# Small vectors, conditions, signal, router and filter inputs as a few column arrays, with the head of the Hyena mixer reordered

## The chip, the core and the metric

The kernel runs on one core of one Trainium2 chip, as one launch. The metric is the device time of one execution in microseconds (us). Inputs lie in the device's main memory when the execution begins, and laying them out in another order on the host, before the launch, is not in the time.

## What is computed

One inference step of a two-layer model on two token streams, in float32: 128 context tokens and 256 latent tokens of width 1024. The streams are kept side by side as 384 token columns. Layer 0 mixes tokens with a bidirectional Hyena long convolution, layer 1 with a bidirectional RG-LRU scan, and each is followed by a mixture of 16 experts (two per token). Each sub-layer is preceded by an RMS norm and modulated by vectors that come from the condition vectors `c` and `c_ctx`:

```
silu_c = silu(cond)
for i in range(2):
    mod = (silu_c @ ada_w[i] + ada_b[i])          # 1024 x 6144 weights
    sh1, sc1, g1, sh2, sc2, g2 = split(mod, 6)
    h = rms_norm(x, norm_mix[i]) * (1 + sc1) + sh1
    m = hyena_mixer(h) if i % 2 == 0 else rglru_mixer(h)
    x = x + g1 * m
    h = rms_norm(x, norm_moe[i]) * (1 + sc2) + sh2
    x = x + g2 * moe_ffn(h)                       # scores, top-2 experts, w1, w3, w2
```

The Hyena filter comes from a small network on fixed positional features, `h = sin(freq * (z @ f_w1 + f_b1))`, `h = sin(freq * (h @ f_w2 + f_b2))`, `h @ f_w3`. Its output is multiplied by a decaying window, normalised, and taken to its spectrum.

## The kernel before, in words

Each engine runs its own instruction list, and the lists are ordered by hand. Semaphores tie them: `wait_ge` holds back one engine's list, and `then_inc` releases. Two engines issue DMAs: SyncE (the rows SPq) and ScalarE (the rows ACTq). A DMA issued by ScalarE stands in ScalarE's list, ahead of the arithmetic that follows it.

**SyncE** loads the two condition vectors as 8 rows each and the identity (lines 353 to 356), the third filter weight `w3` in two halves (L365), and then the stream of weight pieces of 1 MB: eight `ada_w` pieces at once, then `hy_w_in` and further `ada_w` pieces, each after a wait on `ada_mm` or `in_mm0`, which TensorE raises when it is done with a piece's buffer (L374 to L391). After that come the expert weights of 2 MB each (L344).

**ScalarE** first issues ten small DMAs for the filter network (L439 to L444; three vectors of 64 values, each loaded twice, four bytes a partition), then the two signals into `h` (L446, L447), the constants (L448), the window (L449) and the cosine tables `lags` (L450). It computes the sigmoid of the conditions (L452), issues 16 DMAs that bring the small vectors as rows of 128 values into `hT` (L463), then the router weight with 64 bytes a row (L465), and the router bias spread over all partitions (L466). Only then does the filter network's first `sine` begin (L475 to L482): an `Identity` activation into `f_arg` (L478), a range reduction on VectorE (`reduced`, L1245 to L1258), and the `Sin` (L481). Then four evictions of transposed signal tiles (L472), the second `sine`, two copies that build `stack` (L488, L489), the eight squares of the first norm (L495) and its square root (L497).

**TensorE** transposes the conditions (L755), waits for all ten filter DMAs, does the first filter matmul, `ada(0, 1)`, the transposes of the signal (24 tiles of 128x128, from `h` to PSUM), the second filter matmul, the four transposes of the small vectors, `ada(2)`, and `filter_rows(0)`, which needs `stack` and `w3`. `ada(n)` multiplies the conditions with one 1 MB piece: 4 matmuls, 8 records in the trace. In `mixer0` (L923 on) follow `norm_sums(0)`, which needs the eight squares, `ada(3)`, `spectrum(0)`, `norm_spread(0)`, `filter_sums(0)`, `ada(4)`, `filter_rows(1)`, `ada(5, 6, 7)`, `mod_columns(0)`, `spectrum(1)`, `filter_sums(1)`, and then 24 `in_tile`s with the rest interleaved. A matmul helper records all matmuls at L743 and all transposes at L747.

**VectorE** multiplies conditions and sigmoid (L1214), does the two range reductions, four of the eight evictions of the signal (L1263), the evictions of the small vectors into `VT` (L1267), clears four columns of `stack` (L1269), and then multiplies each `filter_rows` result by the window (L1324).

The five PSUM banks from 3 on are handed out in the order of `pool_plan` (L180 to L206). The eight signal tiles head that order.

Of the kernel before, what the change touches and what calls it, by code (L numbers as in the profile page):

```python
# [11 lines left out]
ALU = mybir.AluOpType  # L12
# [3 lines left out]
P = 128  # L16
# [30 lines left out]
BLOCK_ROWS = (120, 88, 80, 112)  # L47
NVEC = 16
# [134 lines left out]
def pool_plan():  # L183
# [11 lines left out]
    order = [("dve" if k % 2 else "act", ("x", k)) for k in range(KD)]  # L195
    order += rows(0) + spectrum(0) + [("dve", ("sums", 0))] + rows(1) + mod(0) + spectrum(1) + [("dve", ("sums", 1))]
# [14 lines left out]
def program(nc, A, y_prompt, y_sample, new_state):  # L211
    where, (pool, pool_order, pool_count) = plan(), pool_plan()
    with ExitStack() as ctx:
# [33 lines left out]
        c_rows = hT[0:16, 4 * P:5 * P]  # L247
# [18 lines left out]
        rbias = small[:, 46:62]  # L266
        fcols = small[:, 62:66]
# [72 lines left out]
        def _(sp):  # L340
# [95 lines left out]
        def _(act):  # L436
            a = nc.scalar

            act.dma_start(features, A["feats"]).then_inc(S("f_in"), 16)  # L439
            act.dma_start(f_w1, A["hy_f_w1"][0]).then_inc(S("f_in"), 16)  # L440
            for d in range(2):
                act.dma_start(f_w2[:, 64 * d:64 * d + 64], A["hy_f_w2"][0]).then_inc(S("f_in"), 16)
                for i, name in enumerate(("hy_f_b1", "hy_f_freq", "hy_f_b2")):
                    act.dma_start(fcols[64 * d:64 * d + 64, i:i + 1], A[name][0].rearrange("(p o) -> p o", o=1)) \  # L444
                        .then_inc(S("f_in"), 16)
            act.dma_start(h[:, 0, :], A["x_prompt"][0]).then_inc(S("x_in"), 16)  # L446
            act.dma_start(h[:, 1:3, :], A["x_sample"][0].rearrange("(t p) d -> p t d", p=P)).then_inc(S("x_in"), 16)  # L447
            act.dma_start(cst[:, P:NCOL], A["cst"][:, P:NCOL]).then_inc(S("cst_in"), 16)  # L448
            act.dma_start(window, A["window"]).then_inc(S("win_in"), 16)  # L449
            act.dma_start(lags, A["lag"]).then_inc(S("win_in"), 16)  # L450
            act.wait_ge(S("cond_mm"), 1)
            a.activation(pre[:, 0, 0:16], PS[:, 2, 0:16], ACT.Sigmoid).then_inc(S("c_sig"), 1)  # L452

            stage = hT[:, 0:4 * P].rearrange("p (b c) -> p b c", b=4)
            vectors = [(0, HB, A["hy_b_in"]), (0, HW, A["hy_conv_w"][0]), (0, HCB, A["hy_conv_b"]),
                       (1, SKIP, A["hy_f_skip"][0]), (1, RB, A["rg_b_in"]), (1, RW, A["rg_conv_w"][0]),
                       (1, RCB, A["rg_conv_b"]), (1, LAM, A["rg_lambda"][0]), (2, BA, A["rg_ba"][0]),
                       (2, BX, A["rg_bx"][0]), (2, ST, A["state_rglru"][0, 0]), (2, NMIX, A["norm_mix"]),
                       (2, NMOE, A["norm_moe"]), (3, ADAB, A["ada_b"]), (3, BO, A["hy_b_out"]),
                       (3, BO + 8, A["rg_b_out"])]  # L460
            for b, at, src in vectors:
                src = src.rearrange("k (r c) -> (k r) c", c=P)
                act.dma_start(stage[at:at + src.shape[0], b, :], src).then_inc(S("rows_in"), 16)  # L463
            act.wait_ge(S("zeroed"), 1)
            act.dma_start(rw[:, :, 0:NE], A["router_w"].rearrange("(k p) e -> p k e", p=P)).then_inc(S("rw_in"), 16)  # L465
            act.dma_start(rbias, A["router_bias"].partition_broadcast(P)).then_inc(S("rw_in"), 16)  # L466
# [7 lines left out]
            def sine(i, parts, dst):  # L474

                act.wait_ge(S("f_mm"), i + 1)
                act.wait_ge(S("f_fb"), i + 1)
                a.activation(f_arg[0:parts, :], PS[0:parts, 1, 0:N], ACT.Identity, bias=fcols[0:parts, 3:4],  # L478
                             scale=fcols[0:parts, 1:2]).then_inc(S("f_arg"), 1)
                act.wait_ge(S("f_red"), i + 1)  # L480
                a.activation(dst, f_arg[0:parts, :], ACT.Sin).then_inc(S("f_sin"), 1)  # L481

            sine(0, 64, f_h1)
            for k in range(0, KD, 2):
                emptied(("x", k), xc[:, k, :])
# [5 lines left out]
            def norm_root(tag, sem, value):  # L491
                for n, k in enumerate(NORM_ORDER[tag]):
                    if sem is not None:
                        act.wait_ge(S(sem), value + n)
                    a.activation(h_ch[:, k, :], xc[:, k, :], ACT.Square).then_inc(S("sq"), 1)  # L495
                act.wait_ge(S("ss_mm"), tag + 1)
                a.activation(rs, PS[:, NORM_BANK[tag], 0:96], ACT.Sqrt, bias=eps, scale=1.0 / D).then_inc(S("rms"), 1)  # L497
# [12 lines left out]
            def norm(tag, sem, value):  # L510
                norm_root(tag, sem, value)
                modulate(tag)
# [69 lines left out]
            def mixer0():  # L582
                act.wait_ge(S("pl_mm"), pool["x", KD - 1][0] + 1)
                act.wait_ge(S("pl_dve"), pool["x", KD - 1][2])
                act.wait_ge(S("pl_act"), pool["x", KD - 2][2])
                norm_root(0, None, 0)
# [154 lines left out]
        def _(pe):  # L741
# [12 lines left out]
            pe.wait_ge(S("c_in"), 48)  # L754
            tr(PS[:, 2, 0:16], c_rows).then_inc(S("cond_mm"), 1)  # L755

# [99 lines left out]
            stage = hT[:, 0:4 * P].rearrange("p (b c) -> p b c", b=4)  # L856
            pe.wait_ge(S("c_ready"), 1)
            pe.wait_ge(S("f_in"), 16 * 10)
            mm(PS[0:64, 1, 0:N], f_w1, features, True, True).then_inc(S("f_mm"), 1)
            ada(0, 1)  # L860
            pe.wait_ge(S("x_in"), 32)
            for k in range(KD):
                bank = take(("x", k))
                for t in range(NT):
                    last = tr(PS[:, bank, P * t:P * t + P], h[:, t, P * k:P * k + P])
                last.then_inc(S("pl_mm"), 1)
            pe.wait_ge(S("f_sin"), 1)
            mm(PS[:, 1, 0:N], f_w2, f_h1, True, True).then_inc(S("f_mm"), 1)
            pe.wait_ge(S("rows_in"), 16 * NVEC)
            for b, n in enumerate(BLOCK_ROWS):  # L870
                tr(PS[:, 0, P * b:P * b + n], stage[0:n, b, :]).then_inc(S("VT_mm"), 1)
            ada(2)
            pe.wait_ge(S("w3_in"), 32)
            pe.wait_ge(S("f_stack"), 2)
            filter_rows(0)
            pe.wait_ge(S("cst_in"), 16)
            pe.wait_ge(S("win_in"), 32)
            pe.wait_ge(S("VT_done"), 4)
# [44 lines left out]
            def mixer0():  # L923
                norm_sums(0)
                ada(3)
                spectrum(0)
                norm_spread(0)
                filter_sums(0)
                ada(4)
# [4 lines left out]
                filter_sums(1)  # L934
                norm_ready(0)
# [96 lines left out]
            def router(l):  # L1032
                pe.wait_ge(S("rw_in"), 32)
# [170 lines left out]
        def _(dve):  # L1204
# [7 lines left out]
            link(v.memset(cT[:, :, :], 0.0))  # L1212
            dve.wait_ge(S("c_sig"), 1)
            v.tensor_tensor(cT[:, :, 0:2], PS[:, 2, 0:16].rearrange("p (s k) -> p k s", s=2),  # L1214
                            pre[:, 0, 0:16].rearrange("p (s k) -> p k s", s=2), ALU.mult).then_inc(S("c_ready"), 1)
            v.memset(rw[:, :, :], 0.0).then_inc(S("zeroed"), 1)
# [30 lines left out]
            def reduced(i, parts):  # L1247
# [3 lines left out]
                v.tensor_tensor(fcols[:, 3:4], fcols[:, 1:2], fcols[:, 2 * i:2 * i + 1], ALU.mult) \  # L1251
# [8 lines left out]
            dve.wait_ge(S("f_in"), 16 * 10)  # L1260
            reduced(0, 64)
            for k in range(1, KD, 2):
                v.tensor_copy(xc[:, k, :], PS[:, source(("x", k)), 0:N]).then_inc(S("pl_dve"), 1)  # L1263
            reduced(1, P)
            for b, n in enumerate(BLOCK_ROWS):
                dve.wait_ge(S("VT_mm"), 4)
                v.tensor_copy(VT[:, b, 0:n], PS[:, 0, P * b:P * b + n]).then_inc(S("VT_done"), 1)  # L1267
# [50 lines left out]
            def filter_rows(i):  # L1318
                cs = slice(HALF * (i % 2), HALF * (i % 2) + HALF)
                if i:  # L1320
                    dve.wait_ge(S("pl_mm"), pool["K", i - 1, NT - 1, 1][0] + 1)
                for t in range(NT):
# [456 lines left out]

_INS = ["x_prompt", "x_sample", "state_rglru", "c", "c_ctx", "ada_w", "ada_b", "norm_mix", "norm_moe", "norm_final",  # L1780
        "hy_w_in", "hy_b_in", "hy_conv_w", "hy_conv_b", "hy_f_w1", "hy_f_b1", "hy_f_freq", "hy_f_w2", "hy_f_b2",
        "hy_f_w3", "hy_f_skip", "hy_w_out", "hy_b_out", "rg_w_in", "rg_b_in", "rg_conv_w", "rg_conv_b", "rg_wa",
        "rg_ba", "rg_wx", "rg_bx", "rg_lambda", "rg_w_out", "rg_b_out", "router_w", "router_bias", "moe_w1",
        "moe_w3", "moe_w2"]
_OUTS = [(1, CTX, D), (1, LAT, D), (1, 1, 2, D)]


# [12 lines left out]
```

## Time and profile before

| | us |
|---|---|
| median of 3 runs | 1823.98 |
| lowest, highest | 1819.24, 1826.66 |
| profiled execution, own time | 1817.12 |
| its span | 1815.3 |
| TensorE busy in the span | 1598.4 (88%) |
| VectorE, ScalarE busy | 705.9 (39%), 333.4 (18%) |
| mean granted TensorE clock | 0.954 of full |

The span runs from the first to the last instruction of the profiled execution, and all times of rows are counted from its start. One matmul of float32 operands gives two records. A busy engine is one that executes instructions other than waits and DMA issues, so ScalarE is idle in the rows while it issues DMAs, though its list can't go on. The page ranks waits by who released them, and a wait for several semaphores is put down to the one that came last.

### The profile page before, as it was taken

To read this page: it belongs to the slowest core of one execution; us is meant where nothing else is said; L and a number is where in the kernel's file an instruction comes from. 1 tells how busy PE (TensorE), PEld (TensorE's weight loads), DVE (VectorE), ACT (ScalarE), POOL (GpSimd) and SP (SyncE) were. 2 spreads that over 40 slices of the span, in tenths; PEclk is the share of its full clock that TensorE was granted. 3 is DMA by queue.
4 is the path that set the end of the run, shared out by engine and by line. 5 is a ranking of instruction groups with operands and counts; after the bars stand their busy time and mean duration, and the time that the engine had idled before them with its cause. 6 is when DMAs were issued, how large, how long until landed. Compare 5 with 4: busy or idle time off the path is not lost.

```text
span 1815.3 us, 21681 instructions
## 1 busy us (share of the span) xinstructions
PE 1598.4 (88%) x7939; PEld 703.9 (39%) x7940; DVE 705.9 (39%) x2042; ACT 333.4 (18%) x543; POOL 0.2 (0%) x4
## 2 busy tenths in 40 slices
PE   2999999987888889998889789896898898998996
PEld 1455555553333333333333355453332333333332
DVE  1422555433324243433333347724332343334342
ACT  1433222111011111101010248512110111010111
POOL 0000000000000000000000000000000000000000
PEclk7899999998999999999999989997999999999998
DMA  9126666650687999999949521412799995999993
GB/s 329 39 101 232 235 243 246 251 205 27 238 318 280 374 403 380 388 397 384 404 184 404 194 90 47 185 47 105 300 406 384 378 405 211 403 391 386 380 404 148
DMA packets 135562, 495.73 MB, mean 273 GB/s; under 512 B 6547, under 2 KB 23524, under 8 KB 128996
## 3 DMA queue, kind: packets, MB, share of 16 engines
q1 hardware_dynamic: 131536, 487.68, 69.3%
q10 hardware_dynamic: 3988, 7.54, 1.1%
q8 instruction: 25, 0.41, 0.1%
q14 instruction: 13, 0.11, 0.0%
HBM read 493.62 MB, written 1.58 MB: 273 GB/s over the span
## 4 chain that ended last, share of the span: by engine, by line
PE 52%; DMA 34%; DVE 5%; ACT 3%; SPq 2%; ACTq 2%; issue 2%; DVEq 0%
PE PS L743 49%; DMA halves<-in_moe_w 34%; PE PS L747 2%; SPq L344 2%; ACTq L463 1%; DVE xc L1683 1%; ACT hT L506 1%; ACTq L466 1%; DVE misc L1503 0%; DVE halves L1503 0%; DVE halves L1496 0%; DVE halves L1494 0%; ACTq L444 0%; DVE halves L1495 0%; DVE hT L1731 0%
## 5 line engine op out<-in xcount | busy, mean ns | idle before, releaser
L743 PE MATMUL PS<-halves,hT 128*64 128x512 f32 x3072 | 701.8, 611 | 87.0 <-DMA halves<-in_moe_w 56.4
L743 PEld LDWEIGHTS PS<-halves,hT 128*64 128x64 f32 x3072 | 225.8, 140 | 531.2 <-issue 446.8
L743 PE MATMUL PS<-hT,halves 128*128 128x384 f32 x640 | 218.4, 497 | 12.2 <-ACT acc L617 6.5
L1683 DVE SCALAR_TENSOR_TENSOR xc<-PS,MOD,xc 128x128 f32<-128x128 f32 x592 | 195.8, 409 | 37.4 <-PE PS L743 37.4
L743 PEld LDWEIGHTS PS<-hT,halves 128*128 128x128 f32 x640 | 121.5, 193 | 110.3 <-issue 20.8
L1731 DVE TENSOR_TENSOR hT<-hT,PS 128x512 f32<-128x512 f32 x32 | 22.0, 687 | 357.7 <-ACT hT L519 357.7
L519 ACT ACTIVATE hT<-PS 128x512 f32<-128x512 f32 x32 | 19.1, 597 | 533.9 <-PE PS L743 533.9
L743 PE MATMUL PS<-h,hT 128*64 128x512 f32 x408 | 108.0, 670 | 3.4 <-DVE hT L1675 3.4
L1740 DVE COPY misc<-PS 128x512 f32<-128x512 f32 x32 | 22.1, 692 | 226.3 <-PE PS L743 226.3
L743 PE MATMUL PS<-hT,misc 64*128 64x384 f32 x512 | 91.2, 495 | 6.4 <-DVE misc L1740 6.4
L743 PE MATMUL PS<-acc,halves 128*128 128x384 f32 x256 | 83.1, 486 | 0.7 <-ACT pre L564 0.7
L747 PEld LDWEIGHTS PS<-cst,hT 128*128 128x128 f32 (+1 forms) x413 | 44.6, 144 | 88.8 <-issue 80.9
L747 PE MATMUL PS<-cst,hT 128*128 128x128 f32 (+1 forms) x413 | 69.4, 291 | 5.2 <-DMA cst<-in_cst 3.5
L539 ACT ACTIVATE hT<-PS 128x512 f32<-128x512 f32 x32 | 19.1, 597 | 254.2 <-PE PS L747 254.2
L743 PEld LDWEIGHTS PS<-acc,halves 128*128 128x128 f32 x256 | 48.5, 190 | 34.9 <-ACT pre L564 1.3
L743 PEld LDWEIGHTS PS<-hT,misc 64*128 64x128 f32 x512 | 46.8, 186 | 38.8 <-DVE misc L1740 14.0
L743 PEld LDWEIGHTS PS<-h,hT 128*64 128x64 f32 x408 | 29.4, 151 | 56.5 <-issue 56.5
L1307 DVE SCALAR_TENSOR_TENSOR h<-pre,VT,h 128x127 f32<-128x127 f32 (+1 forms) x80 | 29.6, 412 | 52.6 <-ACT h L568 32.6
L743 PE MATMUL PS<-halves,cT 128*32 128x512 f32 x384 | 49.8, 636 | 0.0
L743 PE MATMUL PS<-cst,halves 128*128 128x256 f32 (+2 forms) x288 | 46.6, 320 | 0.0
L519 ACT ACT_TABLE_LOAD x32 | 41.1, 1283 | 30.1 <-issue 30.1
L743 PEld LDWEIGHTS PS<-cst,halves 128*128 128x128 f32 x288 | 42.7, 191 | 5.8 <-issue 1.4
(237 smaller groups left out, 1123.4 us busy)
## 6 DMA issues: line engine op xcount, KB each, us to landing
halves<-in_moe_w SPq DMA_DIRECT2D x192, 2048.0 KB, 18.2
halves<-in_ada_w SPq DMA_DIRECT2D x48, 1024.0 KB, 6.5
halves<-in_hy_w_in SPq DMA_DIRECT2D x12, 1024.0 KB, 5.2
halves<-in_rg_w_in SPq DMA_DIRECT2D x4, 2048.0 KB, 16.0
halves<-in_hy_w_out SPq DMA_DIRECT2D x4, 1024.0 KB, 8.0
halves<-in_rg_w_out SPq DMA_DIRECT2D x2, 2048.0 KB, 10.2
halves<-in_rg_wa SPq DMA_DIRECT2D x1, 2048.0 KB, 21.7
halves<-in_rg_wx SPq DMA_DIRECT2D x1, 2048.0 KB, 22.1
```

Of the source, the lines that this page charges most:

```text
L344: sp.dma_start(dst, src).then_inc(S(f"w_ready{where[key][0]}"), 16)
L463: act.dma_start(stage[at:at + src.shape[0], b, :], src).then_inc(S("rows_in"), 16)
L466: act.dma_start(rbias, A["router_bias"].partition_broadcast(P)).then_inc(S("rw_in"), 16)
L506: ins = a.activation(hT3[:, k, cs], hT3[:, k, cs], ACT.Identity, bias=MOD[:, l, 8 * sh + k, s:s + 1], scale=MODA[:, tag, k, s:s + 1])
L519: a.activation(hid, PS[:, 2, :], ACT.Sigmoid).then_inc(S("sig"), 1)
L539: a.activation(xT, PS[:, 1, :].rearrange("p (c m) -> p c m", m=P), ACT.Copy).then_inc(S("xT"), 1)
L743: return nc.tensor.matmul(out, lhsT, rhs, start=start, stop=stop)
L747: return nc.tensor.transpose(out, in_, ident[0:n, 0:n])
L1307: last = v.scalar_tensor_tensor(o, i, weight, o, ALU.mult, ALU.add)
L1683: ins = v.scalar_tensor_tensor(xc[:, k, cs], PS[:, bank, cs], MOD[:, l, 8 * G2 + k, s:s + 1], xc[:, k, cs], ALU.mult, ALU.add)
L1731: ch.link(v.tensor_tensor(hid, hid, PS[:, 2, :], ALU.mult))
L1740: v.tensor_copy(yo, PS[:, 6, :]).then_inc(S("yo"), 1)
```

## The change

The host lays the small inputs out as the kernel wants them on the chip. `VT` (128 partitions, four blocks of 128 columns) now comes by one DMA of 256 KB from one array. It also holds the filter network's three vectors, the conditions (already one column per 128 values) and the router bias spread over the partitions. The signal comes by one DMA of 1.5 MB, transposed, straight into `xc`; the router weight by one of 128 KB, padded; and the filter features with the two small weights by one of 144 KB. The transposes of conditions, signal and small vectors on TensorE are gone, and so are their evictions. ScalarE issues 6 DMAs ahead of its arithmetic instead of 33, and SyncE issues the filter inputs and the signal ahead of `w3` and the eight `ada_w` pieces.

The order changes around them. ScalarE does the first `argument`, four squares (after `x_in`), the first `Sin`, four squares, the second `argument` and `Sin`, and the copies. TensorE does both filter matmuls, `norm_sums(0)`, `filter_rows(0)`, `ada(0)`, `spectrum(0)`, `norm_spread(0)`, `filter_sums(0)`, `ada(1, 2, 3)` and `ada(4)`; from there on its order is as before. The wait for constants splits in three (`ones_in`, `lag_in`, `cst_in`), and VectorE waits for the window itself.

```diff
-            for n, name in enumerate(("c_ctx", "c")):
-                src = A[name] if n == 0 else A[name][0]
-                sp.dma_start(c_rows[8 * n:8 * n + 8, :], src.rearrange("(r c) -> r c", c=P)).then_inc(S("c_in"), 16)
-            sp.dma_start(ident, A["cst"][:, 0:P]).then_inc(S("c_in"), 16)
+            sp.dma_start(hT[0:64, 640:1216], A["filter_in"]).then_inc(S("f_in"), 16)
+            sp.dma_start(xc[:, :, :], A["x"]).then_inc(S("x_in"), 16)
...
+            act.dma_start(VT[:, :, :], A["vectors"]).then_inc(S("v_in"), 16)
+            act.dma_start(cst[:, 0:3 * P], A["cst"][:, 0:3 * P]).then_inc(S("ones_in"), 16)
             act.dma_start(window, A["window"]).then_inc(S("win_in"), 16)
-            act.dma_start(lags, A["lag"]).then_inc(S("win_in"), 16)
...
+            act.dma_start(lags, A["lag"]).then_inc(S("lag_in"), 16)
+            act.dma_start(cst[:, 3 * P:NCOL], A["cst"][:, 3 * P:NCOL]).then_inc(S("cst_in"), 16)
+            act.dma_start(rw[:, :, :], A["router_cols"]).then_inc(S("rw_in"), 16)
+            act.wait_ge(S("v_in"), 16)
+            a.activation(pre[:, 0, 0:16], cond, ACT.Sigmoid).then_inc(S("c_sig"), 1)
...
+            argument(0, 64)
+            act.wait_ge(S("x_in"), 16)
+            squares(0, NORM_ORDER[0][0:4])
             sine(0, 64, f_h1)
-            for k in range(0, KD, 2):
-                emptied(("x", k), xc[:, k, :])
+            squares(0, NORM_ORDER[0][4:8])
+            argument(1, P)
             sine(1, P, stack[:, 0, :])
...
-            ada(0, 1)
-            pe.wait_ge(S("x_in"), 32)
-            for k in range(KD):
-                bank = take(("x", k))
...
             def mixer0():
+                pe.wait_ge(S("f_sin"), 1)
+                mm(PS[:, 1, 0:N], f_w2, f_h1, True, True).then_inc(S("f_mm"), 1)
+                pe.wait_ge(S("ones_in"), 16)
                 norm_sums(0)
-                ada(3)
+                pe.wait_ge(S("w3_in"), 32)
+                pe.wait_ge(S("f_stack"), 2)
+                filter_rows(0)
+                pe.wait_ge(S("c_ready"), 1)
+                ada(0)
+                pe.wait_ge(S("lag_in"), 16)
                 spectrum(0)
                 norm_spread(0)
                 filter_sums(0)
+                ada(1, 2, 3)
                 ada(4)
...
+                pe.wait_ge(S("cst_in"), 16)
                 norm_ready(0)
```

## Rows read from the trace of the kernel before

**Rows 1.** Windows: us; busy of PE, PEld, DVE, ACT, POOL; clock; DMA share; GB/s

```profile
0.00:10.00 10.00, 0.28 (x1) 0.19 (x2) 0.29 (x2) 0.57 (x2) 0.20 (x4) 1.00 0.75 185
10.00:20.00 10.00, 2.29 (x6) 0.49 (x10) 0.66 (x5) 0.91 (x2) 0.00 (x0) 1.00 1.02 409
20.00:30.00 10.00, 4.11 (x22) 1.71 (x15) 0.00 (x0) 0.00 (x0) 0.00 (x0) 0.84 1.02 421
30.00:40.00 10.00, 2.15 (x11) 1.74 (x9) 0.34 (x1) 1.02 (x2) 0.00 (x0) 0.50 1.01 422
50.00:60.00 10.00, 8.35 (x18) 3.40 (x21) 3.98 (x10) 6.07 (x12) 0.00 (x0) 0.62 0.00 1
60.00:80.00 20.00, 20.00 (x139) 10.76 (x138) 8.66 (x16) 6.44 (x9) 0.00 (x0) 0.91 0.00 1
300.00:340.00 40.00, 40.00 (x185) 21.43 (x184) 20.89 (x41) 9.21 (x16) 0.00 (x0) 1.00 0.58 211
```

**Rows 2.** Chain of waits, first 200 us: start, us, engine and line

```profile
28.91 9.95 ACTq L466
38.96 0.68 ACT hT L478
```

**Rows 3.** Timeline, 0 to 75 us: start, us, engine, line, instruction, what ended idleness

```profile
7.49 0.45 ACTq L447 DMA_DIRECT2D h<-in_x_sample  x1
...
8.96 0.45 ACTq L450 DMA_DIRECT2D halves<-in_lag  x1
9.44 1.28 ACT L452 ACT_TABLE_LOAD   x1 [9.29 <-issue]
...
10.74 0.18 ACT L452 ACTIVATE pre<-PS 128x16 f32<-128x16 f32 x1
...
38.96 0.67 ACT L478 ACTIVATE hT<-PS,small 64x384 f32<-64x384 f32 x1 [28.04 <-issue]
39.65 1.28 ACT L481 ACT_TABLE_LOAD   x1
...
41.99 0.52 ACT L481 ACTIVATE hT<-hT 64x384 f32<-64x384 f32 x1 [1.06 <-DVE hT L1258]
...
45.06 1.65 PE L743 MATMUL PS<-hT 64*128 64x384 f32 x2
...
51.45 3.41 ACT L495 ACTIVATE h<-xc 128x384 f32<-128x384 f32 x8
...
51.65 8.31 PE L743 MATMUL PS<-halves,stack 128*128 128x512 f32 x12 [2.22 <-issue]
```

**Rows 4.** Timeline, TensorE: the norm's sums, then weight pieces

```profile
59.88 1.53 PE L743 MATMUL PS<-h,cst 128*32 128x96 f32 x64
...
61.23 1.04 PE L743 MATMUL PS<-halves,cT 128*32 128x512 f32 x8
...
47.49 1.94 PE L743 MATMUL PS<-halves,cT 128*32 128x512 f32 x8
```

**Rows 5.** Timeline after 75 us: three weight pieces, an input piece's DMA, the first `in_tile`

```profile
82.47 2.78 PE L743 MATMUL PS<-halves,cT 128*32 128x512 f32 x24
...
84.45 1.23 SPq L385 DMA_DIRECT2D halves<-in_hy_w_in  x2
...
97.98 5.41 PE L743 MATMUL PS<-hT,halves 128*128 128x384 f32 x16
```

**Rows 6.** DMA issues, 0 to 160 us: count, KB each, us from issue to landing

```profile
misc<-in_window ACTq DMA_DIRECT2D x1, 1536.0 KB, 31.8
cst<-in_cst ACTq DMA_DIRECT2D x1, 1229.0 KB, 26.1
...
h<-in_x_sample ACTq DMA_DIRECT2D x1, 1024.0 KB, 21.2
halves<-in_lag ACTq DMA_DIRECT2D x1, 640.0 KB, 32.8
```

**Rows 7.** The page, chain that ended last: shares of the span by line

```profile
PE PS L743 49%; DMA halves<-in_moe_w 34%; PE PS L747 2%; SPq L344 2%; ACTq L463 1%; DVE xc L1683 1%; ACT hT L506 1%; ACTq L466 1%; DVE misc L1503 0%; DVE halves L1503 0%; DVE halves L1496 0%; DVE halves L1494 0%; ACTq L444 0%; DVE halves L1495 0%; DVE hT L1731 0%
```

More of the change, by code:

```diff
@@ L46 @@
 ADAB, BO = 0, 96
-BLOCK_ROWS = (120, 88, 80, 112)
-NVEC = 16
+FCOL, COND, RBIAS = 120, 88, 80
 IN_ORDER = tuple(range(KD))
@@ L193, in pool_plan @@
     mod = lambda g: [("dve", ("mod", g))]
-    order = [("dve" if k % 2 else "act", ("x", k)) for k in range(KD)]
-    order += rows(0) + spectrum(0) + [("dve", ("sums", 0))] + rows(1) + mod(0) + spectrum(1) + [("dve", ("sums", 1))]
+    order = rows(0) + spectrum(0) + [("dve", ("sums", 0))] + rows(1) + mod(0) + spectrum(1) + [("dve", ("sums", 1))]
     order += rows(2) + spectrum(2) + [("dve", ("sums", 2))] + rows(3) + spectrum(3) + [("dve", ("sums", 3))]
@@ L265, in program @@
         rnorm = small[:, 6:38].rearrange("p (i b s) -> p i b s", i=UNITS, b=4)
-        rbias = small[:, 46:62]
-        fcols = small[:, 62:66]
+        rbias = VT[:, 2, RBIAS:RBIAS + NE]
+        fcols = VT[:, 0, FCOL:FCOL + 3]
+        f_bias = small[:, 65:66]
+        cond = VT[:, 1, COND:COND + 16]
         def tok3(at):
@@ L437, in _ @@
             a = nc.scalar
[L439 to L445, printed above, removed]
@@ L454, in _ @@
[L454 to L460, printed above, removed]
@@ L461, in _ @@
[L461 to L466, printed above, removed]
+            act.dma_start(VT[:, :, :], A["vectors"]).then_inc(S("v_in"), 16)
@@ L472, in emptied, with argument, sine, squares @@
                 a.activation(dst, PS[:, 3 + u % 5, 0:dst.shape[1]], ACT.Copy).then_inc(S("pl_act"), 1)
-            def sine(i, parts, dst):
+            def argument(i, parts):
                 act.wait_ge(S("f_mm"), i + 1)
                 act.wait_ge(S("f_fb"), i + 1)
-                a.activation(f_arg[0:parts, :], PS[0:parts, 1, 0:N], ACT.Identity, bias=fcols[0:parts, 3:4],
+                a.activation(f_arg[0:parts, :], PS[0:parts, 1, 0:N], ACT.Identity, bias=f_bias[0:parts, :],
                              scale=fcols[0:parts, 1:2]).then_inc(S("f_arg"), 1)
+            def sine(i, parts, dst):
                 act.wait_ge(S("f_red"), i + 1)
                 a.activation(dst, f_arg[0:parts, :], ACT.Sin).then_inc(S("f_sin"), 1)
+            def squares(tag, ks, sem=None, value=0):
+                for n, k in enumerate(ks):
+                    if sem is not None:
+                        act.wait_ge(S(sem), value + n)
+                    a.activation(h_ch[:, k, :], xc[:, k, :], ACT.Square).then_inc(S("sq"), 1)
+            argument(0, 64)
+            act.wait_ge(S("x_in"), 16)
+            squares(0, NORM_ORDER[0][0:4])
             sine(0, 64, f_h1)
-            for k in range(0, KD, 2):
-                emptied(("x", k), xc[:, k, :])
+            squares(0, NORM_ORDER[0][4:8])
+            argument(1, P)
             sine(1, P, stack[:, 0, :])
@@ L489, in _, with norm_root @@
             a.activation(stack[64:P, 1, :], stack[64:P, 0, :], ACT.Copy, scale=-1.0).then_inc(S("f_stack"), 1)
[L491 to L495, printed above, removed]
+            def norm_root(tag):
                 act.wait_ge(S("ss_mm"), tag + 1)
@@ L510, in norm @@
             def norm(tag, sem, value):
-                norm_root(tag, sem, value)
+                squares(tag, NORM_ORDER[tag], sem, value)
+                norm_root(tag)
                 modulate(tag)
@@ L582, in mixer0 @@
             def mixer0():
[L583 to L586, printed above, removed]
+                norm_root(0)
                 filter_abs(0)
@@ L854, in inverse @@
                     last.then_inc(S("pl_mm"), 1)
-            stage = hT[:, 0:4 * P].rearrange("p (b c) -> p b c", b=4)
-            pe.wait_ge(S("c_ready"), 1)
-            pe.wait_ge(S("f_in"), 16 * 10)
+            pe.wait_ge(S("f_in"), 16)
             mm(PS[0:64, 1, 0:N], f_w1, features, True, True).then_inc(S("f_mm"), 1)
-            ada(0, 1)
-            pe.wait_ge(S("x_in"), 32)
-            for k in range(KD):
-                bank = take(("x", k))
[L864 to L878, printed above, removed]
             def norm_sums(tag):
@@ L1032, in router @@
             def router(l):
-                pe.wait_ge(S("rw_in"), 32)
+                pe.wait_ge(S("rw_in"), 16)
                 for kk in range(2):
@@ L1250, in reduced @@
                     dve.wait_ge(S("f_arg"), 1)
[L1251 removed]
+                v.tensor_tensor(f_bias, fcols[:, 1:2], fcols[:, 2 * i:2 * i + 1], ALU.mult) \
                     .then_inc(S("f_fb"), 1)
@@ L1321, in filter_rows @@
                     dve.wait_ge(S("pl_mm"), pool["K", i - 1, NT - 1, 1][0] + 1)
+                else:
+                    dve.wait_ge(S("win_in"), 16)
                 for t in range(NT):
@@ L1778 @@
 X_COMBINE = ((0, 4), (2, 0), (4, 5), (6, 7), (1, 6), (3, 1), (5, 5), (7, 7))
[L1780 to L1783, printed above, removed]
+_INS = ["ada_w", "norm_final", "hy_w_in", "hy_f_w3", "hy_w_out", "rg_w_in", "rg_wa", "rg_wx", "rg_w_out", "moe_w1",
@@ L1793 @@
     arrays = {name: np.ascontiguousarray(inputs[name]) for name in _INS}
-    arrays["cst"], arrays["feats"], arrays["window"], arrays["lag"] = constants()
+    arrays["cst"], features, arrays["window"], arrays["lag"] = constants()
+    arrays["vectors"], arrays["x"], arrays["router_cols"], arrays["filter_in"] = laid_out(inputs, features)
     A = {name: nc.dram_tensor(f"in_{name}", a.shape, F32, kind="ExternalInput").ap() for name, a in arrays.items()}
```

41 lines of the change are left out of this document (25 added, 16 removed).

## The prediction

> **What bounds the kernel now.** I read the windows first. From 60 us on TensorE is busy without a gap up to 340 us (first and last of these windows [rows 1]), while in the first 50 us it is nearly idle and the DMA engines are full: 1.85 + 4.09 + 4.21 + 4.22 = 14.4 MB by 40 us (GB/s times 10 us each [rows 1]). The reader is to see that two things could explain the idle head: transfers that have not come, or a list that can't go on. The chain of waits decides: its pieces before 39 us are ScalarE's own DMA issues, one behind the other, of which the last, the spread router bias, alone took 9.95 us [rows 2]. ScalarE's first activation of the filter network follows at 38.96, idle "issue" before it, not a transfer [rows 3]. From there the chain is the filter network, and TensorE's first `filter_rows` matmul starts at 51.65 [rows 3]. After that TensorE's own work sets the end up to the first norm, and later it shares the chain with the expert weights [rows 7]. Every load after the head is released by a semaphore of TensorE, so nothing later hangs on an absolute time: what the head saves, the end saves.
>
> **Head, removed.** 33 DMAs ahead of ScalarE's arithmetic become 6. At about 0.45 us each (7.49 to 8.96 is three steps, 0.49 apart [rows 3]) plus a slower first, they are issued by about 3.9 us. The table load for the sigmoid, 1.28 us [rows 3], ends near 5.2. The 24 signal transposes, their evictions and those of the vectors go too; they stood inside the head and are in the difference below.
>
> **Head, when the data come.** The two issuing queues share the 16 DMA engines, and rows show how. The DMA of `x_sample` (rows of 4 KB) landed at 7.49 + 21.2 = 28.7 us; that of the constants, issued 0.49 later at about 7.96, landed at 34.1, so 1229 KB (rows of 9.8 KB) took 5.4 us; the window (rows of 12.3 KB), issued at about 8.48, landed 6.2 us later for 1536 KB [rows 3, 6]. That is 233 and 254 GB/s out of some 422 [rows 1]: shares of 0.55 and 0.60, which are 9.8 / (9.8 + 8.2) and 12.3 / (12.3 + 8.2) with the other queue's `ada_w` rows of 8.2 KB. So each engine takes one row from each queue in turn. Applied to the new order (each DMA has 8 rows per engine, the filter inputs and each half of `w3` have 4; 26 KB per us and engine; data from about 2.6 us, an estimate between the issue at 1 and 5.5, at which the 1.85 MB of the first ten microseconds would have run at full pace):
> - `vectors`: 4 x 2.3 + 4 x 12.3 + 8 x 2 = 74 KB per engine, lands near 5.5.
> - signal: 4 x 2.3 + 8 x 12.3 + 8 x 2 + 4 x 1.5 = 130 KB, near 7.6; with a tail I take 8.0.
> - `w3` near 12, window near 15.5, `lags` near 19.5, the `ada_w` pieces from 17 to 39 us.
>
> **Head, the new chain.** Sigmoid, product, two clears and the bias product follow the vectors: about 6.5. `argument` 0.67 [rows 3] ends at 7.2, before the signal. From the signal at 8.0: four squares 3.41 / 2 = 1.7 [rows 3], table load 1.28, `Sin` 0.52, ends at 11.5. The range reduction (39.63 to about 41.97, 2.3 us [rows 3]) runs beside it. Four squares more to 13.3; the second filter matmul (1.65 [rows 3]) lies under them. Then `argument` 0.7, reduction 2.3, `Sin` 0.5, two copies and the clear 1.15: 18.0. TensorE starts `filter_rows(0)` near 18.2. From the first `argument` to there: 11.7 us, against 12.7 before (51.65 - 38.96 [rows 3]), plausible as transposes go and squares come in. **The head brings 51.65 - 18.2 = 33.4 us.** Bounds: with the signal at 7 it is 34.4; were the signal to get only half the bandwidth (1.57 MB at 211 GB/s from 2.6 on) it lands at 10.1 to 10.5, and 31; with data only from 5.5, 30.5.
>
> **Norm sums.** They ran behind `filter_rows(0)` from 59.88 to 61.23 [rows 4]; now they fall in the wait for `stack`, between 13.3 and 18.2. That takes 1.35 us off TensorE's path. If the cover went (squares late by more than 3.4 us), these 1.35 us would be back.
>
> **Weight pieces moved onto the path.** `ada(0)`, `ada(1)` and `ada(2)` ran while TensorE was idle anyway; now they stand in its busy stretch. At the high level three pieces take 2.78 us [rows 5]; one at the low level took 1.94 [rows 4]. `ada(0)` replaces `ada(3)` ahead of `spectrum(0)` (1.04 us [rows 4]), and `ada(1, 2, 3)` is added after `filter_sums(0)`: cost 2.8 us net, bound 0 to 5.8 (all three at the low level; nothing, were TensorE to wait there for something else).
>
> **Waits.** `filter_rows(0)` on TensorE and VectorE needs the window from 19 us (comes near 15.5); `spectrum(0)` starts near 18.2 + 8.3 [rows 3] + 1.0 = 27.5 and needs `lags` (19.5); `ada(0)` needs its piece near 26.5 (17); `ada(1)` near 40 (22); `ada(5, 6, 7)` near 50 (39). Cost 0. What is late next if the issuing is gone: no transfer, but the filter network's serial hops between ScalarE and VectorE. The `hy_w_in` pieces are asked for when `ada(6)` and `ada(7)` end (84.45) and used at 97.98 [rows 5]; both move alike. ScalarE's first square waits for the signal, and behind it in its list stands the `Sin`, for which TensorE's second filter matmul waits: this is the one added wait on the path, and it is in the chain above.
>
> **Clock.** The clock is 0.50 from 30 us on, and 0.62 in the window of 50 to 60, at full again by 60 to 80 mostly (0.91), after TensorE had been busy from 51.65 [rows 1, 3]. The 1.00 of the first windows was not what the head ran at: its few pieces ran at the pace of the low level. The new kernel should likewise run `filter_rows(0)` at 1.2 GHz and rise to 2.4 GHz near its end: no gain and no loss. At the high level from the start it would gain some 2 us.
>
> **Table load on the path.** The one for `Sin` follows the squares now. The load at 39.65 begins 0.02 us after the activation before it, and the one at 9.44 is followed by its activation at 10.74: 1.28 us and nothing around it [rows 3]. The Trainium skill (ScalarE: Activation LUTs, section What ACT_TABLE_LOAD costs) counts a drain of 1380 ns beside each load of 1283 ns. By the page the head would be 1.4 us longer and the gain 30.5 us; by the rows it is 31.9, and I take the rows.
>
> **Sum.** 33.4 + 1.35 - 2.8 = 31.9 us less. The profiled execution took 1817.1 us, so 1785.2 on its own scale. The median of the three timed runs is 6.9 us above it (1824.0), so the forecast is 1785.2 + 6.9 = 1792.
>
> **Rivals.**
> - *The transfers are the bound anyway.* Speaks for it: the same 15 MB at 422 GB/s need until 38 us or so, and ScalarE's queue finished last: `lags` at 8.96 + 32.8 = 41.8, the window at 40.3 [rows 3, 6]. Were the new window to come no earlier than 40.3, VectorE's six products would end near 44.7, and `spectrum(0)`, which began at 62.2, would begin there: 17.5 us gained, less 2.8, so 14.7: 1809. Against: these two were behind 1.5 MB of signal and 1.2 MB of constants and were issued at 8.5; now they are issued near 2.
> - *The signal is late*, behind a half share for the window: it lands at 12 and the head is 4 us longer: 1796. Against: the window is third in its queue.
> - *Clock high from the first row*: 1790.
> - *Slower: the expert weights stream more slowly.* With 43 input arrays replaced by 19, the weight arrays may lie elsewhere in memory. Each load of an expert's weights is waited for some 22 us, and such waits are 34% of the chain, 617 us [rows 7]. A stream 5.2% slower costs 32 us and eats the gain; from 6.6% on the kernel is slower by more than 9 us; at 8% it costs 49: 1841. Against: bytes, row sizes and issue order of these loads are untouched.
> - *The change doesn't do what it says*: if squares needed another table than the sigmoid or the sine, up to three loads of 1.28 us would join the head: 1796. Before, squares follow a `Sin` with no load between.
>
> **How the numbers follow.** Forecast 0.78, transfers 0.08, signal late or more table loads 0.08 together, clock high 0.03, slower 0.03. The forecast's own range, from the bounds of the head (30.5 to 34.4), of the pieces (0 to 5.8) and the spread of the runs before (1819 to 1827), is 1784 to 1800. The late signal lies inside it; the transfers' case at 1809 I leave out. A measurement of this kernel tells 0.5%, 9 us, from no change. Faster 0.94; within 0.5% 0.03 (a weight stream some 5% slower, or transfers and clock both against it); slower 0.03.
>
> **What would show it.** In the changed profile: ScalarE's first `Identity` near 6.5 to 7 us; the first `Sin` near 11; TensorE's 12 records of `filter_rows(0)` beginning near 18; no idle time of TensorE between there and the first `in_tile`, which begins near 66; DMA share full up to 39 us; expert loop unchanged. Wrong would be: idle TensorE ahead of `spectrum(0)` or `ada(1)`, released by a DMA; squares that end after 15 us; or a head that is right with an end that has not moved.

## The result, and the profile after

| | before | changed |
|---|---|---|
| median of the first comparison, us | 1822.9 (4 runs, 1819.2 to 1826.7) | 1772.5 (4 runs, 1772.3 to 1773.0) |
| measured again | 1823.0 (17 runs, 1808.8 to 1831.8) | 1774.6 (6 runs, 1770.2 to 1778.0) |
| profiled execution, own time | 1817.1 | 1772.6 |

The ratio is 0.972, with a 95% interval of 0.970 to 0.974: the change takes 50 us, of which the forecast named 32. The measured time lies 20 us under the forecast of 1792 and 11 us under its range, which began at 1784. Two things hide in that one number: the head brought less than forecast, and something that the forecast had not counted brought 20 us more.

**The head.** Timeline of the changed kernel: start, us, engine, line, instruction, and what ended the idle time before it.

```profile
7.33 0.67 ACT L455 ACTIVATE hT<-PS,small,VT 64x384 f32<-64x384 f32 x1 [0.76 <-DVE small L1219]
...
16.59 1.76 ACT L466 ACTIVATE h<-xc 128x384 f32<-128x384 f32 x4 [8.60 <-DMA xc<-in_x]
18.37 1.28 ACT L460 ACT_TABLE_LOAD   x1
19.67 0.52 ACT L460 ACTIVATE hT<-hT 64x384 f32<-64x384 f32 x1
...
21.81 2.79 PE L725 MATMUL PS<-h,cst 128*32 128x96 f32 x64
...
26.87 7.17 PE L725 MATMUL PS<-halves,stack 128*128 128x512 f32 x12 [2.27 <-DVE stack L1231]
...
47.24 5.34 PE L725 MATMUL PS<-halves,cT 128*32 128x512 f32 x32
...
73.38 5.41 PE L725 MATMUL PS<-hT,halves 128*128 128x384 f32 x16
```

The issuing is gone, as forecast: `argument` begins at 7.33 us (before: 38.96 [rows 3]). (The six DMA issues took ScalarE until 5.0 us and not until 3.9; the wait that follows covers this.) But ScalarE then waits 8.60 us for the signal, which lands at 16.6 us and not at 8.0. TensorE starts `filter_rows(0)` at 26.87 and the first `in_tile` at 73.38, so it is 24.8 and 24.6 us ahead of before [rows 3, 5].

Windows of the changed kernel (columns as in [rows 1]), first in the head, then over 14 experts of layer 0's loop, from the second expert's table load to the last one's; below it the same stretch of the kernel before.

```profile
12.00:14.00 2.00, 0.00 (x0) 0.00 (x0) 0.00 (x0) 0.00 (x0) 0.00 (x0) 1.00 0.91 228
14.00:16.00 2.00, 0.00 (x0) 0.00 (x0) 0.00 (x0) 0.00 (x0) 0.00 (x0) 1.00 1.05 234
...
461.69:946.14 484.45, 437.95 (x2370) 165.30 (x2368) 175.43 (x573) 51.90 (x78) 0.00 (x0) 0.99 0.91 362
```

```profile
485.89:979.46 493.57, 443.97 (x2370) 166.91 (x2368) 175.43 (x573) 51.88 (x78) 0.00 (x0) 0.97 0.91 355
```

The same 2370 matmul records take 484.45 us instead of 493.57. The changed kernel is 24.2 us ahead at the beginning of this stretch and 33.3 at its end; from there to the end of the span it is another 11.2, of which the same stretch of layer 1's loop has 7.5 (493.40 against 500.93 us); that makes 44.5. So 16.7 of the 20.3 us that came behind the head lie in these two stretches of the expert loops, where no line was changed. The page's row on the expert matmuls says more (out<-in, count; busy us, mean ns; idle before them, and of it by the releaser); first the changed kernel, then the one before:

```profile
L725 PE MATMUL PS<-halves,hT 128*64 128x512 f32 x3072 | 691.6, 604 | 79.6 <-DMA halves<-in_moe_w 49.1
```

```profile
L743 PE MATMUL PS<-halves,hT 128*64 128x512 f32 x3072 | 701.8, 611 | 87.0 <-DMA halves<-in_moe_w 56.4
```

They waited 7 us less for weights, and ran 10 us shorter, since the granted clock was low less often (0.99 against 0.97 in the loop of layer 0). Two explanations offered themselves: the loops fell more kindly against the clock, or the weights came faster.

### The profile page after: what moved, and what is told of

Same layout as the page of the kernel before. It is cut to its first block, busy times and chain, and to the rows that moved or that the text cites. A ratio compares the mean times of both kernels' runs of the same rounds, so it can differ in the third digit from the quotient of the medians.

```text
span 1770.8 us, 21581 instructions
## 1 busy us (share of the span) xinstructions
PE 1577.1 (89%) x7910; PEld 696.1 (39%) x7911; DVE 702.8 (40%) x2033; ACT 332.2 (19%) x539; POOL 0.2 (0%) x4
## 4 chain that ended last, share of the span: by engine, by line
PE 52%; DMA 36%; DVE 5%; ACT 3%; SPq 2%; issue 2%; DVEq 0%; ACTq 0%
PE PS L725 50%; DMA halves<-in_moe_w 35%; SPq L344 2%; PE PS L729 2%; DVE xc L1647 1%; DMA xc<-in_x 1%; ACT hT L490 1%; DVE misc L1467 0%; DVE halves L1467 0%; DVE halves L1458 0%; DVE halves L1460 0%; DVE halves L1459 0%; DVE hT L1695 0%; ACT h L466 0%; ACT hT L504 0%
## 5 line engine op out<-in xcount | busy, mean ns | idle before, releaser
L725 PE MATMUL PS<-halves,hT 128*64 128x512 f32 x3072 | 691.6, 604 | 79.6 <-DMA halves<-in_moe_w 49.1
L729 PEld LDWEIGHTS PS<-cst,hT 128*128 128x128 f32 x408 | 44.0, 143 | 85.5 <-issue 80.4
L729 PE MATMUL PS<-cst,hT 128*128 128x128 f32 x408 | 68.3, 291 | 1.7 <-DVE hT L1681 1.7
```

The source lines that it names most:

```text
L725: return nc.tensor.matmul(out, lhsT, rhs, start=start, stop=stop)
L729: return nc.tensor.transpose(out, in_, ident[0:n, 0:n])
```

## The experiments

The short names of theories below: *clock* (phase of the loops against low clock), *place* (where the weight arrays lie). No run read an address. What the runs vary is the order in which input arrays are declared, and how many bytes are declared ahead of the large ones; that this moves them in memory is inferred.

**Unused arrays back at their old places.** The program is the changed one; it only declares the old arrays too.

```diff
-_INS = ["ada_w", "norm_final", "hy_w_in", ...]
+_INS = ["x_prompt", "x_sample", "state_rglru", "c", "c_ctx", "ada_w", "ada_b", ...]   # all of before, most unused
```

> The changed kernel, which also declares every input array of the kernel before, unused, in the old order, so that the expert weights are declared at their old places. Theory 1 (the gain beyond the head comes from fewer stretches of low TensorE clock in the expert loops, a matter of phase): nothing changes, 1772 us, expert loops 484 and 534 us long as in the changed kernel. Rival (the expert weights lie elsewhere in memory and stream better): the loops go back to 494 and 545 us, about 1792 us.

Measured: 1794.5 us (4 runs, 1786.2 to 1799.8), the loop of layer 0 at 493.6 us. That is the rival's value. The clock theory took its first blow: with arrays that nothing reads, 20 us of the gain were lost.

**The head's gain given back by a delay.**

```diff
             squares(0, NORM_ORDER[0][0:4])
+            for n in range(46):
+                a.activation(acc_ch[:, n % 8, :], xc[:, n % 8, :], ACT.Square).then_inc(S("idle"), 1)
+                act.wait_ge(S("idle"), n + 1)
```

> The changed kernel with 46 more squares of 0.53 us on ScalarE ahead of the first Sin, so that TensorE reaches the first filter_rows about 24.6 us later, where the kernel before reached it. Theory 1 (low clock in the expert loops depends on the phase of the loops in time): the loops fall back to the length of before, about 494 and 545 us, and the whole takes 1772 + 24.6 + 20 = 1817 us, or anything between 1797 and 1820, as the phase falls. Rival (placement of arrays): loops stay at 484 and 534, exactly 1797 us.

Measured: 1800.3 us (1795.7 to 1804.3). The first expert's table load stood at 429.2 us, 24.7 us behind that of the changed kernel run again (404.5); 1774.6 + 24.7 = 1799.3. So time saved in the head is time saved at the end, one for one, and at this one other phase the 20 us stayed.

**A filler ahead of the wait for weights**, in both kernels.

```diff
+                        if k == 4:
+                            for n in range(4):
+                                mm(PS[0:30, 3, :], cT[:, 0, 2:32], weight(l, 1)[:, n, 0:HALF], False, False)
```

> The kernel before with 4 matmuls of 512 columns (zeros added into an open sum, 1.8 us) on TensorE ahead of its wait for the second half of w1 and w3, in each expert. Theory 1 (low clock follows from the wait of 1.5 to 3 us there): the low stretches in the expert loops go, the loops take about 31.0 us per expert, 485 and 535 us, and the whole 1822 - 20 = about 1800 us. Rival (the stream of weights itself is slower in this kernel): no change or slower, 1820 to 1830 us, with loops of 494 and 545 or more.

> The changed kernel with the same 4 matmuls per expert. Theory 1: most of the remaining low stretches in the expert loops go (4 and 5 of them, some 3 us each), about 1750 to 1760 us, and its distance to the kernel before with the same matmuls is the head's 24.6 us and no more. Rival (weight stream): 1772 us or slower, and the distance between the two stays 45 to 50 us.

Measured: 1854.8 and 1826.6 us. Both expectations missed: the filler took 3.6 us per expert, not 1.8 (four matmuls with 30 columns of weights took 3.62 us, about as long as eight with 64 columns in the rows around them, 3.5), and made TensorE the bound at 33.0 us per expert. That is of use. First the kernel before, then the changed one, over the same 14 experts:

```profile
487.52:997.51 509.99, 484.92 (x2482) 175.52 (x2480) 175.55 (x573) 51.90 (x78) 0.00 (x0) 0.99 0.88 344
```

```profile
461.55:971.52 509.97, 484.90 (x2482) 175.63 (x2480) 175.53 (x573) 51.90 (x78) 0.00 (x0) 0.99 0.87 344
```

Where TensorE is the bound, the loops of both are equal to 0.02 us, and the whole differs by 28.2 us: the head, and nothing more. The surplus in time exists only where the loop waits for weights. The slower packets are there even so: the mean 4 KB packet of the loops took 0.1665 and 0.1666 us in the kernel before (layer 0, layer 1) and 0.1658 and 0.1656 in the changed one.

**One matmul instead of four**, and the changed kernel again.

> The changed kernel unaltered, again. If the fewer low-clock stretches of its expert loops (four in each, against seven and seven before) are a matter of how the loops happen to fall in time in one session, its median leaves 1772.5 us and lies between 1772 and 1797 us with a spread of several us, as the spread of the version with the arrays at their old places (1786 to 1800). If they belong to this program, it takes 1772.5 us again within 1 us.

> The kernel before with one matmul of 512 columns per expert (zeros added, 0.9 us) ahead of the wait for the second weight halves; four of them took 3.6 us each expert and made TensorE the bound at 33.0 us per expert with no low clock. Low-clock theory: the wait shrinks from 1.5 to 2.5 us to 0.6 to 1.6 us and most low stretches in the loops go: about 31.0 us per expert, the loops 484 and 493 us or less, the whole about 1800 us. Rival (low clock comes whatever TensorE does there): loops 494 and 501 us, the whole at 1820 us or above.

> The changed kernel with the same one matmul per expert. Low-clock theory: 1765 to 1773 us, and 25 to 28 us below the kernel before with one matmul, which is the head alone. Rival (the expert loops of the changed kernel are faster for a reason of their own): the distance is 40 us or more.

Measured: 1774.6 us (1770.2 to 1778.0) for the changed kernel, 1823.3 and 1782.4 with the filler. The changed kernel keeps its 20 us, but not as the expectation had it: the median is 2.1 us off and not within 1, and the runs spread over 8 us. The stretches of low clock vary from run to run, too. This time its profile has seven and five in the two loops (24 and 17 us) where the first had four and four, and the loops take 489.6 and 495.3 us. So the four against seven of the first two profiles were in part chance, and this run alone doesn't separate the theories; the ones below do.

The distance with one matmul is 40.9 us, the rival's side of the line: with the wait shortened but not gone, most of the surplus is back. The page's rows, the kernel before and then the changed one:

```profile
L743 PE MATMUL PS<-halves,hT 128*64 128x512 f32 x3072 | 688.8, 601 | 72.0 <-DMA halves<-in_moe_w 40.4
```

```profile
L725 PE MATMUL PS<-halves,hT 128*64 128x512 f32 x3072 | 687.1, 600 | 57.6 <-ACT hT L521 27.8
```

Here the matmuls run nearly equally long and the clock is low nearly equally long in the two loops, 31 and 27 us, and still the kernel before needs 15.8 us more for them (1000.8 against 985.0). The difference is waiting: 40.4 us for weights against 27.0 (the second row names only its largest releaser, the list of waits has the weights next). The filler also helps neither kernel, so shortening the wait to keep the clock up is no improvement.

**The place tested from the other end.** The kernel before, the same program, with its arrays declared in the changed kernel's order:

```diff
+_FIRST = ["ada_w", "norm_final", "hy_w_in", "hy_f_w3", "hy_w_out", "rg_w_in", ..., "moe_w1", "moe_w3", "moe_w2"]
+_INS = _FIRST + [n for n in _INS if n not in _FIRST]
```

> The kernel before, with its input arrays declared in another order: the twelve large ones first, in the order of the changed kernel, the small ones behind them; the program is the same. Placement theory (some 20 of the 48 us come from where the weight arrays lie): 1823 - 20 = about 1802 us, 1795 to 1808, with the mean time of an expert weight packet at 0.1652 to 0.1658 us instead of 0.1661 to 0.1668, and fewer stretches of low clock in the expert loops. Rival (placement of unused arrays did something else, and the clock's phase makes the 20 us): 1823 us as before.

> The changed kernel with three unused arrays of 256 bytes each declared ahead of the large ones. If it is small arrays ahead of the weights that put them at worse places (alignment), it loses most of the 20 us: 1785 to 1795 us. If it is their order and large distances, it stays at 1770 to 1778 us.

Measured: 1801.1 us (6 runs, 1790.1 to 1810.6) for the first, ratio to the kernel before 0.989 with an interval of 0.985 to 0.993. Mean times of an expert weight packet, worked out from the trace's packet records of the two loops, were 0.1654 and 0.1661 us; the second is 0.0003 above the range expected. Its row on the expert matmuls is that of the changed kernel and not that of before:

```profile
L743 PE MATMUL PS<-halves,hT 128*64 128x512 f32 x3072 | 694.8, 606 | 78.7 <-DMA halves<-in_moe_w 48.1
```

The three tiny arrays changed little: 1777.3 us (1774.3 to 1780.2), inside the range for "no effect".

**Number or place.** The unused arrays moved behind all used ones; and two unused arrays of 0.5 and 1 MB put ahead of all.

```diff
-_INS = ["ada_w", ...]
+_INS = ["x_prompt", "x_sample", "ada_w", ...]
```

> The changed kernel with the same unused arrays as in the run of 1794 us, but declared behind all arrays that it uses. If it is the place of the large arrays that counts, it takes 1770 to 1778 us like the changed kernel. If it is their mere number, 1790 to 1798 us.

> The changed kernel with two unused arrays, of 0.5 and 1 MB, declared ahead of all others. If the place depends on what lies ahead in bytes, 1785 to 1798 us. If it depends on the order of the large arrays among themselves or on small ones between them, 1770 to 1778 us.

Measured: 1775.1 us (1770.6 to 1780.5) with the unused arrays last, 1794.9 us (1790.4 to 1799.0) with 1.5 MB ahead. The latter's rows, the loop of layer 0 and the page's row:

```profile
456.93:951.29 494.36, 443.09 (x2370) 166.35 (x2368) 175.56 (x573) 51.90 (x79) 0.00 (x0) 0.98 0.90 355
```

```profile
L725 PE MATMUL PS<-halves,hT 128*64 128x512 f32 x3072 | 706.7, 614 | 93.2 <-DMA halves<-in_moe_w 62.5
```

So it is not the number of arrays but what is declared ahead of the large ones, and 1.5 MB there is enough to lose 20 us.

**Why the signal was late.** The window's DMA moved to SyncE, behind the signal and `w3`; `w3` as one DMA over 128 partitions; and both.

```diff
-            act.dma_start(window, A["window"]).then_inc(S("win_in"), 16)
+            sp.dma_start(window, A["window"]).then_inc(S("win_in"), 16)      # behind w3
```

```diff
-            for d in range(2):
-                sp.dma_start(w3[64 * d:64 * d + 64], A["hy_f_w3"][0][:, 2 * D * d:2 * D * d + 2 * D] ...
+            sp.dma_start(w3[:, :, :], A["hy_f_w3"].rearrange("p (n c) -> p n c", n=2)) ...   # 128 rows
```

> The changed kernel with the window's DMA issued by SyncE behind the signal and w3 instead of by ScalarE ahead of lags. Theory (the signal lands at 16.6 us because window rows of 12 KB take every second turn of the DMA engines): the signal now alternates with rows of 5 and 9 KB and lands some 3 to 5 us earlier, the first filter_rows starts at 22 to 24 us instead of 26.9, and the end moves by as much, but for the low clock's share of 10 us either way. Rival (the signal's own rate or the slow stretch of the DMA engines from 12 us on sets it): it lands at 14 to 17 us as before.

> The changed kernel with w3 laid out on the host as 128 rows and loaded by one DMA over all 128 partitions instead of two over 64 each. Theory (loads that write only 64 partitions run the DMA engines at some 240 GB/s and hold up what stands beside them, the stretch from 12 us on): the GB/s stay at 400 from 6 us to 36 us, all transfers of the head end 3 to 5 us earlier, the signal lands 1 to 4 us earlier and the whole takes 1769 to 1773 us. Rival (the slow stretch has another cause): 230 to 270 GB/s still stand between 12 and 18 us.

> The changed kernel with both edits: the window's DMA from SyncE behind signal and w3, and w3 as one DMA of 128 rows. The signal lands at 8.5 to 10 us, the window by about 18 us and no longer holds VectorE (it did for 2.7 us with the late window alone), the first filter_rows starts near 19.5 us, the whole takes 1766 to 1771 us. Rival (the window held back is late in another way): 1771 to 1775.

Measured: window late 1770.8 us (1767.8 to 1774.0); `w3` whole 1778.5 (1773.2 to 1782.7); both 1770.5 (6 runs, 1767.5 to 1777.2). The kernel with both, timeline of its head:

```profile
9.57 1.76 ACT L465 ACTIVATE h<-xc 128x384 f32<-128x384 f32 x4 [2.96 <-DMA xc<-in_x]
...
19.85 5.39 PE L724 MATMUL PS<-halves,stack 128*128 128x512 f32 x12 [2.27 <-DVE stack L1230]
```

With the window behind, the signal lands at 9.6 to 9.8 us instead of 11.2 to 16.6 (nine profiles with the changed kernel's order), and `filter_rows(0)` begins near 20, earlier than the 22 to 24 expected. With the window late alone, VectorE then waited 2.7 us for it. `w3` whole alone left the landing at 12.5 us, but took the slow stretch away; its windows:

```profile
12.00:14.00 2.00, 0.00 (x0) 0.00 (x0) 0.00 (x0) 1.51 (x4) 0.00 (x0) 1.00 1.01 419
14.00:16.00 2.00, 0.00 (x0) 0.00 (x0) 0.00 (x0) 1.97 (x4) 0.00 (x0) 1.00 1.05 435
```

So 419 and 435 GB/s stand where the changed kernel had 228 and 234. The kernel before had the same slow stretch, in its first ten microseconds, where the two halves of `w3` moved from 3.4 to about 8.6 us nearly alone:

```profile
4.00:6.00 2.00, 0.00 (x0) 0.00 (x0) 0.00 (x0) 0.00 (x0) 0.00 (x0) 1.00 0.96 225
```

The landing at 12.5 us, later than the 11.2 of some profiles with the slow stretch, also says that `w3` isn't all that makes the signal late. The median of `w3` whole is 4 us above the changed kernel's, with ranges that overlap: the gain that was expected (1769 to 1773) didn't come. Both edits together are 4 us below the changed kernel run again, with overlapping ranges (1767.5 to 1777.2 and 1770.2 to 1778.0): the head is shorter by 1.5 to 7 us in the profiles, the whole is at best 0.2% faster, and I don't call that shown.

**One part of the head alone**, in the kernel before: the router weight's and bias's DMAs issued behind the filter network.

```diff
+            def router_in(): ...      # the two rw_in DMAs, called behind the copies that build stack
```

> The kernel before, with one edit: ScalarE issues the router weight's and the router bias's DMAs behind the filter network instead of ahead of it. The chain of waits charges them 1.3 and 9.95 us of the head. Theory (the head is ScalarE's issuing, the cover is gone behind it): the first argument begins 8 to 11 us earlier unless the signal, which landed at 28.7 us, or the window at 40.3 us is late; with the window at 40.3 the first products of VectorE hold TensorE little, and the whole takes 1812 to 1816 us instead of 1822. Rival (the late transfers hold the head anyway): 1820 us or more.

Measured: 1814.2 us (10 runs), ratio 0.997 with an interval of 0.994 to 0.999 to the kernel before at 1819.8. Timeline:

```profile
27.76 0.67 ACT L479 ACTIVATE hT<-PS,small 64x384 f32<-64x384 f32 x1 [16.74 <-issue]
...
44.87 0.93 PE L750 MATMUL PS<-cst,hT 120*128 120x120 f32 x4 [10.39 <-DMA hT<-in_rg_b_out]
```

ScalarE's first activation moved from 38.96 to 27.76, the 11.2 us that the chain of waits had charged. Only 5.6 came out at the end: TensorE then waited until 44.87 for the small vectors, whose DMAs ScalarE issues behind those of the signal, the constants, the window and `lags`, and `filter_rows(0)` began at 47.60, 4.05 us earlier than before. The issue time and the late landings were two covers, one above the other, and the change had to lift both.

## Why the prediction was wrong

- **The bound of the head: right.** ScalarE's issuing was it. Two of its 33 DMAs alone gave 11.2 us at the first activation.
- **"What the head saves, the end saves": right.** The delay came back one for one (24.7 us in, 25.7 out), and with like places the change is worth 1801.1 - 1774.6 = 26.5 us, with the other places 1823.0 - 1794.5 = 28.5, with TensorE as the bound 28.2.
- **The head's size, 33.4 us: too large by 8.6** (24.8 in the first profile, the worst of all in this; 28.3 when the same kernel ran again, where the signal came at 13.1, and 30.2 at best). The failed term is the signal's landing, 8.0 us. The rule of turns fits the packet records, its start was wrong: I let the signal alternate with `vectors` and `ones` and the window with `w3`. In fact the signal's first rows moved at 3.75 us, when the last row of `vectors` was through (3.2) and those of `ones` nearly so (4.3), so it had the window's rows of equal size beside it for most of its length. By the nine profiles this costs 1.4 us or more (11.2 at best, against 9.6 to 9.8 with the window behind); 9.6 is itself 1.6 later than forecast. I also took the first ten microseconds of the kernel before, 1.85 MB, for full pace after a late start. They ran at 225 and 229 GB/s between 4 and 8 us, with `w3`: the slow stretch was there to be seen. In the changed kernel it lasted from 12 to 22 us. What spreads the landing from 11.2 to 16.6 us stays open. "The signal is late" was a rival at 1796, with the window's share as its cause, which was right in part, and too small a chance. The rest of the chain held: from the signal to `filter_rows(0)` I had 10.2 us, measured 26.87 - 16.59 = 10.3. In the kernel with both edits, where the signal does land at 9.6, it starts at 19.85.
- **Norm sums and weight pieces: right, with luck.** The lead at the first `in_tile` is 24.6 us, from 24.8 at `filter_rows(0)`. Forecast were +1.35 and -2.8. The norm sums did leave the path. The pieces cost 3.5 us (5.27 for `ada(1, 2, 3)` and `ada(4)` together, 1.81 for `ada(4)` before), inside the bound, because a stretch of low clock fell on them; before, it had fallen on `ada(4)` and `filter_rows(1)`, which is now 0.8 us shorter. The other 1.1 us is `filter_rows(0)` at 7.17 us instead of 8.31, since the clock rose 3.6 us after its start and not 5.9. In other profiles it took 8.2 and 5.4: where the clock rises is luck here, and at the high level from the start it is worth 2.9 us, where I had put some 2.
- **The table load: the rows were right.** 18.37 + 1.28 = 19.65, and the `Sin` starts at 19.67. By this, the Trainium skill's drain of 1380 ns (ScalarE: Activation LUTs, What ACT_TABLE_LOAD costs) is not on the path here.
- **The 20 us behind the head: not in the sum.** Here the forecast failed. The sum has no term for the expert loops, the waits stand in it at "Cost 0", and the sign to look for was "expert loop unchanged"; the loops brought 20 us. I had the cause, the weight arrays' place, as the rival "slower", with 3%, and gave it one sign only. The kernel before had a bad place, and the change happened upon a good one. The two misses have opposite signs: the head brought 5 us less than the forecast's 31.9 by the runs with like places (26.5), the loops 20 more. Had the head come as forecast, the miss would have been larger. I also argued "bytes, row sizes and issue order are untouched", which was true and did not bear on it.

What the place does is shown as far as this: the bad places (kernel before, 1.5 MB ahead, old places) wait 56 to 63 us for weights at the expert matmuls, the good ones of the same programs without filler 47 to 54; mean packet times in the loops are 0.1659 to 0.1668 us against 0.1652 to 0.1661, where single loops just overlap. By the median packet (0.160 us in both) and the rate in those microseconds in which the DMA engines are full (410 GB/s in both) there is no difference: it sits in few slow packets. The slowest hundredth of a run's packets begins at 0.26 to 0.30 us with the bad places and at 0.21 to 0.25 with the good ones, with no overlap among the 17 profiles. Half a per cent of 31 us is 0.16 us per expert, 5 us in 32. How the rest comes about is open. An expert's loads take a little longer than TensorE's work (an estimate of 33.0 - 3.6 = 29.4 us from the runs with four filler matmuls, against the 31 us that an expert takes without); TensorE waits for the second halves, the clock at times falls, and the next matmuls run slower, as here in the changed kernel, 8.79 us against 7.09 with the clock up:

```profile
611.59 7.09 PE L725 MATMUL PS<-halves,hT 128*64 128x512 f32 x32
620.74 8.79 PE L725 MATMUL PS<-halves,hT 128*64 128x512 f32 x32 [2.06 <-DMA halves<-in_moe_w]
```

An expert with such a stretch mostly takes 33 to 34.5 us instead of 31. Over both loops and without filler the clock was low for 48 to 55 us with the bad places and for 27 to 44 us with the good ones, so the clock goes with part of the surplus. But it isn't needed for it: with one filler matmul the low stretches were nearly equal and the loops still 15.8 us apart, of which the waits for weights have 13.4, or 0.5 us at each of 27. Why a wait grows by more than the mean packet does, and what about the place matters, no run here tells.

## What to carry to other kernels

Ask what a change does to the memory layout of everything it doesn't touch. Adding, dropping or merging input arrays changes what lies ahead of the large ones, and where a loop sits on the balance between transfers and compute, this alone was worth 1.1%, and it could as well have been a loss. To tell such an effect from the edit's own, declare the old arrays unused at their places, or reorder the arrays of the old kernel: two cheap runs. And when a head is freed of issuing, look at which rows of the other queue the first needed transfer alternates with from its first row on, and whether the trace of before has a stretch in which the DMA engines are full and move half of what they do elsewhere.

## What the runs showed of the hardware that I had not expected

- The order in which input arrays are declared, and what lies ahead of the large ones: 1801.1 against 1821.6 us for one program, 1774.6 and 1775.1 against 1794.5 and 1794.9 for another.
- While two loads over 64 partitions each (1 MB in all) moved, all transfers together ran at 200 to 290 GB/s for most of that time, in the kernel before and in the changed one; as one load over 128 partitions the same stretch ran at 419 to 435 GB/s.
- The landing of one and the same transfer, the signal, varied from 11.2 to 16.6 us among nine profiles with the same DMA order.
- Four matmuls with 30 columns of weights took 3.6 us, where eight with 64 columns, in pairs, take 3.5: a lone narrow matmul costs as much as a pair.
